# A fused encoder layer: softmax weights of the first three heads turned by VectorE blocks and a pass through DRAM

## The reference

```python
def attend(blk):
    qn, qr = blk
    s = (jnp.einsum('bqhd,bkhd->bhqk', qn, k_nope) + jnp.einsum('bqhr,bkr->bhqk', qr, k_rope))
    p = jax.nn.softmax(s * MLA_SCALE, axis=-1)
    return jnp.einsum('bhqk,bkhd->bqhd', p.astype(v.dtype), v)
...
mixed = jnp.concatenate([o_mla * jax.nn.silu(gate_mla), o_pool * jax.nn.silu(gate_pool),
                         o_gla * jax.nn.silu(gate_gla)], axis=-1)
return x + jnp.einsum('bse,ed->bsd', mixed, w_out)
```

## Time and profile before

| | |
|---|---|
| median of 3 runs | 753.68 us (753.6 to 753.91) |
| profiled execution | 753.71 us, its span in the trace 751.9 us |
| busy: PE, DVE, ACT, POOL | 99%, 55%, 41%, 29% |
| DMA, mean over the span | 86 GB/s |
| attention in the trace | 398.75 to 617.8 us |

### The profile page before, as it was taken

The page is one execution under the profiler, slowest core; times in us unless marked ns, Lnnn a source line. Parts: engine busy times, 40 slices in busy tenths (PEclk is TensorE's granted clock), DMA queues, the critical chain, the costliest instruction groups (busy, mean ns, idle before and its releaser), DMA issues.

```text
span 751.9 us, 14593 instructions
## 1 busy us (share of the span) xinstructions
PE 741.2 (99%) x6024; PEld 625.3 (83%) x6024; DVE 413.6 (55%) x742; ACT 310.4 (41%) x536; POOL 219.9 (29%) x262
## 2 busy tenths in 40 slices
PE   8999999999999999999999999999999999999996
PEld 6998878878888888888887988888898888888885
DVE  5855867376566542016265667667667754433232
ACT  6654445334433422323224545455546543232221
POOL 3223226366556422123400000000009804322320
PEclk9999999999999999999999999999999999999999
DMA  7513021101122133220243000000043035565441
GB/s 254 182 26 88 28 104 49 30 31 44 59 71 87 71 114 135 90 84 2 63 182 99 15 15 14 15 16 15 15 157 124 0 101 169 194 195 155 138 153 56
DMA packets 40622, 64.70 MB, mean 86 GB/s; under 512 B 4433, under 2 KB 23377, under 8 KB 40562
## 3 DMA queue, kind: packets, MB, share of 16 engines
q1 hardware_dynamic: 34272, 49.61, 20.6%
q10 hardware_dynamic: 6290, 14.23, 4.9%
HBM read 43.58 MB, written 19.27 MB: 84 GB/s over the span
## 4 chain that ended last, share of the span: by engine, by line
PE 94%; DVE 3%; ACT 1%; DMA 1%; issue 0%; POOL 0%; DVEq 0%; POOLq 0%
PE psum L78 24%; PE psum L80 23%; PE psum L79 23%; PE psum L2008 5%; PE psum L1535 4%; PE psum L1999 2%; PE psum L2000 2%; PE psum L1374 2%; PE psum L1254 1%; DVE g_state L1062 1%; PE psum L1404 1%; PE psum L1429 1%; PE psum L1279 1%; PE psum L2028 1%; PE psum L1329 1%; PE psum L1398 1%
## 5 line engine op out<-in xcount | busy, mean ns | idle before, releaser
L78 PE MATMUL psum<-h_hi,z_w_hi 128*128 128x512 f32 x376 | 152.4, 405 | 0.0
L80 PE MATMUL psum<-h_hi,z_w_lo 128*128 128x512 f32 x376 | 146.7, 390 | 0.0
L79 PE MATMUL psum<-h_lo,z_w_hi 128*128 128x512 f32 x376 | 146.6, 390 | 0.0
L78 PEld LDWEIGHTS psum<-h_hi,z_w_hi 128*128 128x128 f32 x376 | 70.6, 188 | 15.9 <-issue 0.7
L80 PEld LDWEIGHTS psum<-h_hi,z_w_lo 128*128 128x128 f32 x376 | 70.6, 188 | 15.4
L79 PEld LDWEIGHTS psum<-h_lo,z_w_hi 128*128 128x128 f32 x376 | 70.7, 188 | 14.0 <-issue 0.7
L78 PE MATMUL psum<-o_w_hi,o_m_hi 128*128 128x512 f32 x184 | 72.5, 394 | 0.0
L80 PE MATMUL psum<-o_w_hi,o_m_lo 128*128 128x512 f32 x184 | 72.3, 393 | 0.0
L79 PE MATMUL psum<-o_w_lo,o_m_hi 128*128 128x512 f32 x184 | 72.2, 392 | 0.0
L1877 ACT ACTIVATE a_weights<-psum,a_bias,mla_q_scale 128x1024 f32<-128x1024 f32 (+1 forms) x48 | 51.1, 1066 | 46.6 <-DVE a_bias L1938 46.4
L805 POOL TENSOR_TENSOR z_w_lo<-z_w_raw,z_w_hi 128x1024 fp32r<-128x1024 f32 x17 | 41.0, 2414 | 94.5 <-ACT z_w_hi L501 92.4
(11 more groups left out here) (258 smaller groups left out, 1533.2 us busy)
## 6 DMA issues: line engine op xcount, KB each, us to landing
z_w_raw<-in_w_z_dram SPq DMA_DIRECT2D x17, 512.0 KB, 3.6
n_x_in<-in_x_dram SPq DMA_DIRECT2D x12, 512.0 KB, 3.7
gates_scratch<-z_gate ACTq DMA_DIRECT2D x24, 256.0 KB, 2.1
o_x_in<-in_x_dram SPq DMA_DIRECT2D x12, 512.0 KB, 3.6
out_dram<-o_y ACTq DMA_DIRECT2D x11, 512.0 KB, 3.1
o_w_raw<-in_w_out_dram SPq DMA_DIRECT2D x8, 512.0 KB, 9.2
rope_scratch<-p_rope_split SPq DMA_DIRECT2D x12, 256.0 KB, 2.6
a_q_rope<-rope_scratch SPq DMA_DIRECT2D x48, 64.0 KB, 1.9
```

What stands on the lines that cost most here:

```text
L78: nc.tensor.matmul(out, a_hi, b_hi, start=first, stop=False)
L79: nc.tensor.matmul(out, a_hi, b_lo, start=False, stop=False)
L80: return nc.tensor.matmul(out, a_lo, b_hi, start=False, stop=last)
```

## The change

For heads 0 to 2 (steps 0 to 35) PE no longer turns the weights. DVE transposes each 32 x 32 block of a tile's exponentials within its 32 partitions, one step behind (`transpose(m - 1)`); ACT stores the result to a DRAM scratch (`store_spread`); SP loads a pair of tiles back with four DMAs that put the blocks on the right partitions, in rows of 1 KB (512 bytes for short tiles), into `turned_lo`; ACT copies the high half five steps behind (`take_high(m - 5)`) and POOL subtracts it in place. Values move to step 2p + 8 for most pairs, outputs to two steps behind them and gathers to one behind that, so that pairs have three slots. Banks 4 and 5, free of turned weights, become a third pair of score banks for these heads; the projections move to other steps and banks. Head 3 is turned by PE as before. As POOL is now taken until step 40, w_out is split from then on, in another order of rows (5, 6, 7, 4, 0 to 3), with the high halves of rows 0 to 3 copied by ACT; its loads use two semaphores, and POOL's gate work moves between them.

Places and order of the steps:

```diff
-TURN_LAG, VALUES_LAG, OUTPUT_LAG, GATHER_LAG = 2, 4, 5, 6
-PROJECT_AT = {5: 0, 7: 1, 9: 2}
...
+LAST_HEAD = (HEADS - 1) * TILES
+SPREAD_PAIRS = LAST_HEAD // 2
+TURN_LAG = 2
+VALUES_AT = tuple(2 * p + 8 for p in range(SPREAD_PAIRS - 2)) + (39, 41, 42, 44, 45, 47, 49, 51)
+LATE_OUTPUTS = SPREAD_PAIRS - 2
+OUTPUT_AT = tuple(m + (2 if p < LATE_OUTPUTS else 1) for p, m in enumerate(VALUES_AT))
+GATHER_AT = tuple(m + 1 for m in OUTPUT_AT)
+PROJECTIONS = {2: (1, 0), 4: (1, 1), 6: (1, 2), 20: (2, 0), 21: (2, 1), 22: (2, 2), 32: (3, 0), 33: (3, 1), 34: (3, 2)}
+MIX_GATES_STEP, HEADS_GATES_STEP = STEPS - 5, STEPS - 2
+SPLIT_FIRST_STEP = STEPS - 2
 FIRST_PRODUCTS = {STEPS: 1, STEPS + 1: 2, STEPS + 2: 1, STEPS + 3: 2, STEPS + 4: 2}
+W_OUT_ORDER = (5, 6, 7, 4, 0, 1, 2, 3)
+W_HI_BY_SCALAR = {44: 0, 45: 1, 47: 2, 48: 3}
+
...
+def score_bank(m):
+
+    return 2 * (m % 3 if m < LAST_HEAD else (m - LAST_HEAD) % 2)
...
+def slot_of(p):
+
+    return p % 3 if p < SPREAD_PAIRS else p % 2
```

SyncE, ahead of the rest of its queue:

```diff
                 load_rope(0, b)
+            for p in range(SPREAD_PAIRS):
+                count = keys_of(2 * p)
+                for n in range(2):
+                    sp.wait_ge(spread_stored[n], 16 * p + 16)
+                if before_in_slot(p):
+                    sp.wait_ge(values_done, before_in_slot(p))
+                for g in range(4):
+                    keys = slice(g * SPREAD, (g + 1) * SPREAD)
+                    sp.dma_start(turned_lo[slot_of(p)][keys, 0:2 * count].bitcast(F32).rearrange("p (x e) -> p x e", x=8),
+                                 spread_dram[count][p % 3].rearrange("t (a p) (g e) -> g p (t a) e", a=4, g=4)[g])\
+                      .then_inc(spread_loaded[p % 3], 16)
+                if p % 2:
```

GpSimd:

```diff
-            for k in range(KT):
-                if k == 6:
+            for m in range(LAST_HEAD):
+                part = portion(m)
+                high, low = turned_hi[slot_of(m // 2)], turned_lo[slot_of(m // 2)]
+                pool.wait_ge(spread_hi_ready, m + 1)
+                nc.gpsimd.tensor_tensor(low[:, part], low[:, part].bitcast(F32), high[:, part].bitcast(F32), ALU.subtract)\
+                  .then_inc(spread_lo_ready, 1)
+            for i, k in enumerate(W_OUT_ORDER):
+                if i == 1:
                     pool.wait_ge(gate_loaded, 16)
                     pool.wait_ge(mix_loaded, 16)
                     multiply(mix, mix_gates).then_inc(first_step, 1)
-                if k == 7:
+                if i == 3:
                     pool.wait_ge(gate_turned, 1)
                     nc.gpsimd.tensor_scalar(mix_gates, mix_gates, 1.0, 0.5, ALU.add, ALU.mult).then_inc(first_step, 1)
                     pool.wait_ge(first_step, 2)
                     multiply(mix, mix_gates).then_inc(first_step, 1)
-                pool.wait_ge(w_out_loaded[k], 16)
-                if k == 5:
-                    pool.wait_ge(scores_done, TILES * (HEADS - 1))
-                for half in range(2):
-                    nc.gpsimd.tensor_copy(keep.w_out_hi[k][half][:, :], keep.w_out[k][:, half * BLK:(half + 1) * BLK])\
-                      .then_inc(w_hi_set, 1)
+                    pool.wait_ge(values_done, SPREAD_PAIRS)
+                if i == 4:
+                    pool.wait_ge(gathered, 3 * TILES + 2)
+                    multiply(of_heads, heads_gates).then_inc(first_step, 1)
+                if i == 6:
+                    pool.wait_ge(gate_opened, 1)
+                    nc.gpsimd.tensor_scalar(heads_gates, heads_gates, 1.0, 0.5, ALU.add, ALU.mult).then_inc(first_step, 1)
+                    pool.wait_ge(first_step, 5)
+                    multiply(of_heads, heads_gates).then_inc(gated, 2)
+                if k >= 4:
+                    pool.wait_ge(w_out_loaded[i % 2], 16 * (i // 2) + 16)
+                    if i == 0:
+                        pool.wait_ge(scores_done, LAST_HEAD)
+                    for half in range(2):
+                        nc.gpsimd.tensor_copy(keep.w_out_hi[k][half][:, :], keep.w_out[k][:, half * BLK:(half + 1) * BLK])\
+                          .then_inc(w_hi_set, 1)
...
+                    if k >= 4:
+                        pool.wait_ge(w_hi_set, 2 * i + half + 1)
+                    else:
+                        pool.wait_ge(scalar_copied, scalar_copy_of(k))
...
-            pool.wait_ge(gathered, 3 * TILES // 2 + 1)
-            multiply(of_heads, heads_gates).then_inc(first_step, 1)
-            pool.wait_ge(gate_opened, 1)
-            nc.gpsimd.tensor_scalar(heads_gates, heads_gates, 1.0, 0.5, ALU.add, ALU.mult).then_inc(first_step, 1)
-            pool.wait_ge(first_step, 5)
-            multiply(of_heads, heads_gates).then_inc(gated, 2)
```

ScalarE, in step m:

```diff
+                if m >= LAST_HEAD + SLOTS:
                     act.wait_ge(turned, TILE_END[m - SLOTS])
-                nc.scalar.activation(weights[:, m % SLOTS, 0:count * P].rearrange("p (a k) -> p a k", k=BLK),
+                nc.scalar.activation(weights[:, weights_slot(m), 0:count * P].rearrange("p (a k) -> p a k", k=BLK),
                                      psum[:, banks, :], ACT.Exp, bias=bias[:, m:m + 1],
                                      scale=keep.q_scale[:, tile:tile + 1], accum_out=total[:, m:m + 1])\
                   .then_inc(exp_done, 1)
 
+            def store_spread(m):
+                count, p = keys_of(m), m // 2
+                act.wait_ge(transposed, m + 1)
+                if m % 2 == 0 and p >= 3:
+                    act.wait_ge(spread_loaded[p % 3], 64 * (p // 3))
+                act.dma_start(spread_dram[count][p % 3, m % 2], spread[m % 2][:, 0:count]).then_inc(spread_stored[m % 2], 16)
+
+            def take_high(m):
+                p = m // 2
+                if m == 0:
+                    for tb in range(TB):
+                        act.wait_ge(front.rope_stored[tb], 64)
+                act.wait_ge(spread_loaded[p % 3], 64 * (p // 3) + 64)
+                nc.scalar.activation(turned_hi[slot_of(p)][:, portion(m)], turned_lo[slot_of(p)][:, portion(m)].bitcast(F32),
+                                     ACT.Copy).then_inc(spread_hi_ready, 1)
...
                 if m < STEPS:
                     exponentials(m)
+                if 1 <= m <= LAST_HEAD:
+                    store_spread(m - 1)
                 for h, b in projected_at(m):
                     project(h, b)
-                for p in pair_at(m, VALUES_LAG):
+                if 5 <= m < LAST_HEAD + 5:
+                    take_high(m - 5)
+                for p in pair_at(m, VALUES_AT):
```

VectorE, in step m:

```diff
+            def transpose(m):
+                count = keys_of(m)
+                dve.wait_ge(exp_done, m + 1)
+                if m >= 2:
+                    dve.wait_ge(spread_stored[m % 2], 16 * (m // 2))
+                nc.vector.transpose(spread[m % 2][:, 0:count].rearrange("p (g j e) -> p j g e", g=4, e=SPREAD),
+                                    weights[:, weights_slot(m), 0:count].rearrange("p (j g e) -> p j g e", g=4, e=SPREAD))\
+                  .then_inc(transposed, 1)
+
...
+                for p in pair_at(m, GATHER_AT):
+                    if p >= SPREAD_PAIRS:
+                        gather(p)
+                if 1 <= m <= LAST_HEAD:
+                    transpose(m - 1)
+                    take_share(m - 1)
                 for h, b in projected_at(m):
                     project(h, b)
-                for p in pair_at(m, VALUES_LAG):
```

TensorE: the slots of the scores, the values, and the loop of steps:

```diff
-                    pe.wait_ge(turned_lo_ready, QUERY_END[h, g // 4])
-                if m >= 2:
-                    pe.wait_ge(exp_done, m - 1)
+                    pe.wait_ge(turned_lo_ready, QUERY_END[h, max(g // 4, 1)])
+                if g == 1 and h:
+                    pe.wait_ge(turned_lo_ready, QUERY_END[h, 2])
+                if m == 2:
+                    pe.wait_ge(turned_lo_ready, QUERY_END[0, 2])
+                if m >= 3:
...
             def values(p):
                 _, first, count = QUERY_TILES[(2 * p) % TILES]
                 if p >= 2:
-                    pe.wait_ge(gathered, p - 1)
-                pe.wait_ge(turned_lo_ready, TILE_END[2 * p + 1])
+                    pe.wait_ge(gathered, 2 * p - 2)
+                if p == 0:
+                    pe.wait_ge(turned_lo_ready, QUERY_END[1, 2])
+                if p < SPREAD_PAIRS:
+                    pe.wait_ge(spread_lo_ready, 2 * p + 2)
+                    high, low = (part[slot_of(p)][:, 0:2 * count * P].rearrange("p (x j e) -> p x j e", x=8, j=count)
+                                 for part in (turned_hi, turned_lo))
+                    high, low = ([part[:, :, k, :] for k in range(count)] for part in (high, low))
+                else:
+                    pe.wait_ge(turned_lo_ready, TILE_END[2 * p + 1])
+                    high, low = ([by_key(part, p)[:, k, :] for k in range(count)] for part in (turned_hi, turned_lo))
...
             pe.wait_ge(front.k_stacked, 16)
             pe.wait_ge(front.w_v_lo_ready, 1)
-            for m in range(STEPS + GATHER_LAG):
```

(45 more changed lines are left out.)

148 lines of the change are left out of this document (85 added, 63 removed).

## The result

The changed kernel takes **749.22 us** (median of 4 runs, 747.33 to 750.29) beside 753.64 us for the kernel before on the same chip: 0.9932 of it, 95% interval 0.9914 to 0.9949. It is faster, by 4.4 us and not by 20, and lies 3 us above my range. The profiled execution took 750.29 us, span 748.5.

What follows compares the result with a forecast made beforehand. The prediction took PE (TensorE), busy for 99% of the span, to bound the kernel. 753.7 - 27 (transposes) + 6.1 (fill) + 1.0 (clock) + 0 (tail) = 733.8 us, range 727 to 746.

Steps and rivals of the forecast that it cites:

- term 2: Fill before the first value products: values of pair 0 wait for the pass through DRAM, +6.1 us.
- term 3: TensorE's clock falls to half rate in the gap that the fill opens, +1 us.
- Term 1: Heads 0 to 2: PE loses 240 of its 320 transposes of weights, 27 us removed.
- The new work: Per head, VectorE 36.2, ScalarE 31.6 and GpSimd 24.5 us with the added instructions, within PE's 44.9.
- rival A: VectorE's transpose takes two passes, 2.3 us each, so VectorE needs 47.2 us a head: 750 us, chance 0.08.
- hidden with some 4 us of room: Pass through DRAM: store 3 us, 1 MB load 6.5, landing at 13, first needed by ScalarE at about 16.7.
- From pair 2 on the parts are ready first: Value products after the fill: from pair 2 on their high and low parts are ready before PE comes.
- Term 4: Tail: GpSimd starts on w_out later, at step 40; zero, with 1 to 2 us of risk near step 48.
- the third slot: Score banks: PE waits for the exponentials of step m-3 instead of m-2, a gain of at most 0.7 us.
- E: The edit moves work but loads come a little late in most pairs, 1 us in 12: 746 us, chance 0.05.
- B: Pass through DRAM is the bound: ScalarE's wait for a load holds back exponentials and scores; 809 us at 150 GB/s, chance 0.07.

Runs made afterwards that it cites:

- half the bytes: The changed kernel with each store and load of the pass through DRAM moving half its bytes from pair 3 on: 742.23 us (0.9842).
- loads by tile: The changed kernel with each tile of a pair loaded by four DMAs of its own as soon as it is stored: 738.21 us (0.9787).
- the latent copy first: The kernel with loads by tile, with ScalarE's copy of a pair's latent values ahead of its rounding of a loaded tile: 738.28 us (0.979).
- the twenty products: The changed kernel with twenty 512-column products without a use in front of the first value products: 747.3 us (0.9922).
- the other layout: The changed kernel with each tile stored by four DMAs on SyncE's queue and loaded by one in 4 KB runs once stored: 737.24 us (0.9781).

## Why the prediction was wrong, step by step

The time is 15.4 us above the forecast. By the account above, 10.0 of them are waits (16.1 us where term 2 had 6.1) and 5.7 the clock (6.7 where term 3 had 1). Splitting the loads gives back 6.8 of the waits and 3.6 of the clock.

- **Term 1, the transposes: right.** 240 fewer, and the kernels in which the way through DRAM is short enough get the gain.
- **The new work: right.** The VectorE transpose takes 1.24 us (I took 1.2, between 1.08 and 2.4; L958, behind the 2.4, isn't the slowest long row, as L1185 takes 4.0 us for 1536), so rival A falls, and that its 750 us is near the measured time is chance. ScalarE's rounding takes 1.06. GpSimd's subtractions are 72.5 us where 24.5 a head were expected; its busy time grows by 67.7, as ScalarE took some of w_out's copies from it.
- **Term 2, the fill: right for pair 0, in part by luck.** Values at 427.72 where the chain gave 428.2, idle 5.5 against 5.9. That VectorE sets the pace is what the trace shows, but its steps are a little shorter than I had them, 2.6 and 4.25 us for 2.8 and 4.4. Pair 0's load landed at 420.9 where I had 419, and ScalarE stood 1.0 us in front of it. The two work against each other. For pair 1 I had 0.9 us and the trace has 2.1.
- **The step that failed: "hidden with some 4 us of room".** It took a store at 3 us and the 1 MB load at 6.5; they took 6.4 and 9.1 for pair 1. That is 6 us more, against 4 of room. The 2.8 us came from three stores of the scalar queue; the trace of before also had three of the same size on SyncE's queue with a median of 5.0, and I took the lower row; here stores and loads run at once, the DMA engines' share reads 1.02 at 307 GB/s in 425:430, where w_out's load in 4 KB runs had 412 at the same share. I had worked out 260 GB/s of need and compared it with 412, not with what the pass reaches in both directions at once. By the Trainium skill ("DMA: Bandwidth & Descriptors", section "Latency and other measured facts") the latency of DRAM access rises under high load. The trace agrees in direction, with 6.6 us for a store that takes 3.6 once the loads are spread out, but it doesn't tell latency from shared bandwidth, and the 7 us that half the bytes are worth speak for bandwidth.
- **The length of the wait by pair was never priced.** I saw that a load waits for both tiles' stores, and counted it as latency alone. It makes 1 MB bursts of what could be two halves, and taking it away is worth 11 us.
- **"From pair 2 on the parts are ready first": wrong, by order.** Even with the loads there, 4.1 us of waits for GpSimd stand at pairs 6, 8, 12 and 14 (7.2 + 2.1 less the fill's 4.6, less 0.6 in the last head). Rounding sits behind the exponentials of a VectorE-paced step, and GpSimd's 2.4 us twice behind that. I had used VectorE's pace for the fill and TensorE's pace for the rest. Where long scores meet the 12 products of a short pair, TensorE needs 4.5 + 1.45 + 0.57 = 6.6 us a pair. VectorE's own work is 2 x 2.58 + 1.25 (latent subtraction and the two steps of the gather, 0.42 each) = 6.4, but with loads by tile it stands another 1.3 to 1.7 us in every such pair for the latent copy, which is on ScalarE behind an exponential and a rounding:

```profile
462.17 0.43 DVE L2101 TENSOR_TENSOR a_latent_lo<-psum,a_latent_hi 128x256 fp32r<-128x256 f32 x1 [1.30 <-ACT a_latent_hi L2031]
```

  So such a pair takes 7.7 to 8.1 us there from maximum to maximum (7.1 with the latent copy first), and TensorE, ahead at first, meets the next pair too early.
- **Term 3, the clock: mechanism right, size wrong.** +1 was for one gap; there are four stretches at half rate, one behind each of the four longest gaps, and it comes to 6.7 us. Its price in the fill alone was not isolated (the twenty products delay the values themselves); over half of the cost went with the gaps themselves (0.1261 us between value products with loads by tile, so 3.1 us).
- **Term 4, the tail, and the third slot: zero, as measured.** With three and two slots it is 749.2 and 748.2, their intervals overlapping. Behind 604 us of the trace TensorE has no wait for another engine that the profile lists. A row of w_out costs GpSimd 3.9 us by rows 7, not 3.7, which changes nothing.
- **Rivals.** E had most of the mechanism, loads a little late in most pairs, at 746 with a chance of 0.05: 10.6 us of later waits, in 8 of the 18 pairs, against its 12. It lacked the clock behind the long ones, and 4.1 of the 10.6 stay with the loads in time. B's place was right as well, ScalarE in front of a load with the exponentials behind it. It decides the sign once the rounding comes a step earlier (762 us), so the changed kernel was one step away from being slower. Giving E and B together 0.12 was the mistake of judgement; the room rested on the two least supported figures of the sum.

The prediction's own time, 733.8 us, is about what the kernel with loads by tile rounded a step earlier takes (734.5), though by another sum (8.3 us idle). The change has that much in it, and two places of its schedule kept it back.

## What to carry to other kernels

When work moves off the bound engine through DRAM, price the landing under the load that the pass itself makes, both directions at once, and try to start each load on one tile as soon as it is stored rather than on a pair. Then walk the ring of in-order queues once at the pace of the slowest engine of that stretch, not of the kernel as a whole. An earlier consumer is a gain only where its data is there: the same one-step move was worth -4 us with split loads and +13 without.

## What the runs showed of the hardware

- The granted clock fell after gaps of 2 us, and not at once: the gap before pair 1 ends at 436.96, the clock is 0.50 in 439:441, with TensorE working without a pause in between, and 1.00 from 442. Behind the fill it was 0.50 in 425:430 and 0.58 in 430:432. It fell behind the gaps of 1.96 and 1.95 us too, and not behind that of 1.63. But it isn't the length of a gap alone: with the other layout a gap of 2.06 us ends at 472.74, and the clock stays:

```profile
474.00:476.00 2.00, 2.00 (x19) 2.00 (x18) 1.97 (x5) 2.00 (x5) 0.58 (x1) 1.00 0.84 292
```

  By the Trainium skill ("TensorE: Matmul & The Clock Gate", the section on the HAM clock gate) the clock comes back after activity; these rows agree.
- A 512 KB store landed in 2.8 us on ScalarE's queue in the kernel before and in 5.0 on SyncE's; in the pass, on ScalarE's queue, in 3.6 to 4.4 with the loads spread and in 5.0 to 6.6 beside loads in bursts of 1 MB.
- The VectorE transpose in blocks of 32 of 1024 fp32 elements a partition took 1.24 us, as long as a maximum over as many (1.21).
